# Interleaving the 512-column and 256-column matmuls of each block product, contraction tile by contraction tile, in a one-core decoder block

## What is computed

```python
h = rms_norm(x, norm_mix_pre)
proj = einsum("btd,dp->btp", h, w_in) + b_in          # input projection, 2048 -> about 11 thousand columns
...                                                    # two recurrent branches, merge, output projection
x = x + rms_norm(mix_out, norm_mix_post)
h = rms_norm(x, norm_ffn_pre)
gate = causal_dwconv(einsum("btd,df->btf", h, ffn_w_gate), ffn_conv_w, ffn_conv_b)
up = einsum("btd,df->btf", h, ffn_w_up)
out = einsum("btf,fd->btd", gelu(gate) * up, ffn_w_down)
x = x + rms_norm(out, norm_ffn_post)
```

## Time and profile before

| | |
|---|---|
| median of three runs | 2742.39 us |
| span of the profiled execution | 2742.6 us |
| TensorE, matmuls | 2709.5 us busy (99%), 14435 instructions |
| TensorE, weight loads | 2315.1 us busy (84%) |
| DVE | 2051.3 us (75%) |
| ACT | 1366.2 us (50%) |
| GpSimd | 365.0 us (13%) |

### The profile page before, as it was taken

How to read it: one execution, slowest core, us unless ns; L and a number is a source line. 1 busy time by engine, 2 the same in 40 slices (tenths; PEclk the granted TensorE clock), 3 DMA queues, 4 the chain that set the end, 5 groups by cost and what they waited for, 6 DMA issues and landing times. The chain is left out here.

```text
span 2742.6 us, 39530 instructions
## 1 busy us (share of the span) xinstructions
PE 2709.5 (99%) x14435; PEld 2315.1 (84%) x14435; DVE 2051.3 (75%) x2374; ACT 1366.2 (50%) x1717; POOL 365.0 (13%) x438
## 2 busy tenths in 40 slices
PE   8999999999999999999989999999999999999998
PEld 7888888888888888888878888888888888888887
DVE  7788888888656554433688787878787888787888
ACT  4365555555543232223565555555555555555554
POOL 1000000000020010000001222222222222222213
PEclk9999999999999999999999999999999999999999
DMA  4344444445434334445625888888888888888876
GB/s 179 116 142 126 142 127 141 127 145 186 156 112 128 91 114 143 138 139 183 215 77 164 186 172 164 169 186 169 164 171 184 169 165 173 183 168 165 174 167 246
DMA packets 463086, 429.67 MB, mean 157 GB/s; under 512 B 14978, under 2 KB 359174, under 8 KB 460184
## 3 DMA queue, kind: packets, MB, share of 16 engines
q1 hardware_dynamic: 401208, 300.98, 36.2%
q0 software_dynamic: 51424, 108.72, 22.8%
q10 hardware_dynamic: 10368, 18.88, 1.8%
HBM read 315.28 MB, written 113.25 MB: 156 GB/s over the span
## 5 line engine op out<-in xcount | busy, mean ns | idle before, releaser
L1953 POOL DMA_DIRECT2D down_sums<-arena x304 | 261.2, 967 | 906.2 <-ACT arena L1688 881.2
L2580 DVE TENSOR_TENSOR sum_ring<-quads 128x1024 f32<-128x1024 f32 x164 | 201.0, 1226 | 169.1 <-PE ps L1139 137.1
L1644 ACT CAST op_ring<-sum_ring 128x1024 fp32r<-128x1024 f32 x164 | 173.0, 1055 | 269.3 <-DVE sum_ring L2580 269.3
L1133 PE MATMUL ps<-hl,op_ring 128*128 128x512 f32 x1064 | 266.1, 392 | 2.6 <-ACT hl L1622 1.6
L1997 DVE TENSOR_TENSOR w_lo<-raw,w_hi 128x2048 fp32r<-128x2048 f32 x68 | 155.7, 2290 | 150.3 <-ACT w_hi L1273 145.1
L1133 PEld LDWEIGHTS ps<-hl,op_ring 128*128 128x128 f32 x1064 | 193.3, 189 | 39.0 <-ACT hl L1622 1.8
L1273 ACT CAST w_hi<-raw 128x2048 fp32r<-128x2048 f32 x69 | 131.6, 1907 | 151.8 <-PE ps L762 108.0
L1688 ACT COPY arena<-ps 128x512 f32<-128x512 f32 x320 | 178.7, 585 | 51.3 <-PE ps L1174 42.9
L2594 DVE TENSOR_TENSOR op_ring<-sum_ring,op_ring 128x1024 fp32r<-128x1024 f32 x164 | 199.9, 1219 | 5.0 <-ACT op_ring L1644 5.0
L1133 PE MATMUL ps<-h,op_ring 128*128 128x512 f32 x792 | 198.0, 392 | 1.6 <-ACT h L1622 1.3
L1172 PE MATMUL ps<-op_ring,act_hi 128*128 128x512 f32 x480 | 187.6, 391 | 0.1
(11 more groups left out here) (394 smaller groups left out, 6043.2 us busy)
## 6 DMA issues: line engine op xcount, KB each, us to landing
down_sums<-arena POOLq DMA_DIRECT2D x320, 256.0 KB, 6.6
quads<-in_w_in SPq DMA_DIRECT2D x116, 512.0 KB, 4.4
quads<-in_ffn_w_gate SPq DMA_DIRECT2D x88, 512.0 KB, 4.7
quads<-in_ffn_w_up SPq DMA_DIRECT2D x88, 512.0 KB, 4.8
quads<-in_ffn_w_down SPq DMA_DIRECT2D x88, 512.0 KB, 7.6
raw<-in_w_in SPq DMA_DIRECT2D x30, 1024.0 KB, 5.5
raw<-in_w_out SPq DMA_DIRECT2D x24, 1024.0 KB, 5.0
projections<-arena ACTq DMA_DIRECT2D x40, 256.0 KB, 3.3
```

Source lines behind the costliest of these rows:

```text
L1133: pe.matmul(ps[:, bank, :], w[0][:, j, :], h[:, j, :, :].rearrange("p r t -> p (r t)"), start=(j == 0 and q not in (M7, M6)), stop=False, ...
L1644: act.copy(op_hi[slot], src).then_inc(op_hi_ready, 1)
L1953: pool.dma_start(dst, src, accum_op=ALU.add).then_inc(acc_added[s], 16)
L2580: dve.tensor_tensor(sum_of(i, pos), quads[:, a, :], quads[:, b, :], ALU.subtract if q in (M7, M6) else ALU.add).then_inc(weights_summed, 1)
```

## The change

In both places the eight long and eight short matmuls of a product are no longer two runs. For each tile `j` the long matmul is followed at once by the short one. The wait for `op_lo_ready` moves ahead of the first short matmul, which is now behind the first long one. The first seven products of the feed-forward keep the old order. No instruction is added or removed; `op_done` is counted up by the last matmul as before.

```diff
@@ in_product
                 for j in range(HALF):
                     pe.matmul(ps[:, bank, :], w[0][:, j, :], IN_MOVING[q](j), start=(j == 0 and q in (P1, P4, P6, P5)), stop=False,
                               skip_group_check=True)
-                pe.wait_ge(op_lo_ready, o + 1)
-                for j in range(HALF):
+                    if j == 0:
+                        pe.wait_ge(op_lo_ready, o + 1)
                     mm = pe.matmul(ps[:, bank, 0:TH], w[1][:, j, :], IN_MOVING[q](j)[:, 0, :], start=False, stop=(j == HALF - 1),
                                    skip_group_check=True)
@@ times_h
-                for j in range(HALF):
+
+                def by_hi(j):
                     pe.matmul(ps[:, bank, :], w[0][:, j, :], h[:, j, :, :].rearrange("p r t -> p (r t)"),
                               start=(j == 0 and q not in (M7, M6)), stop=False, skip_group_check=True)
-                for r in turned_between:
-                    less_hi(r)
-                pe.wait_ge(op_lo_ready, o + 1)
-                for j in range(HALF):
-                    mm = pe.matmul(ps[:, bank, 0:TH], w[1][:, j, :], h[:, j, 0, :], start=False, stop=(j == HALF - 1),
-                                   skip_group_check=True)
+
+                def by_lo(j):
+                    return pe.matmul(ps[:, bank, 0:TH], w[1][:, j, :], h[:, j, 0, :], start=False, stop=(j == HALF - 1),
+                                     skip_group_check=True)
+
+                if isinstance(i, int) and i == 0 and pos < len(SLOT_FIRST):
+                    for j in range(HALF):
+                        by_hi(j)
+                    for r in turned_between:
+                        less_hi(r)
+                    pe.wait_ge(op_lo_ready, o + 1)
+                    for j in range(HALF):
+                        mm = by_lo(j)
+                else:
+                    for j in range(HALF):
+                        by_hi(j)
+                        if j == 0:
+                            pe.wait_ge(op_lo_ready, o + 1)
+                        mm = by_lo(j)
                 mm.then_inc(op_done, 1)
```

## The result

The changed kernel takes 2761.73 us at the median of four runs (2759.95 to 2762.93), the kernel before 2742.61 us in the same comparison: a ratio of 1.0069 with a 95% interval of 1.0056 to 1.0081, 19 us slower. The recorded span is 2760.4 us. This is where the third rival, a stream that never settles, had the time: 2763 us, with a chance of 32%.

The account below looks back on a forecast made before the run. TensorE was taken to bound the kernel in both stretches. From 2742.6 us, 9.7 us less for the pitch of the pairs and 1.7 us more for the wait gave 2734.6 us, with a range of 2712 to 2764 us.

Parts of the forecast that it names:

- the third rival: Input projection and feed-forward: each long matmul pays 7 ns, no short discount; 353.7 ns a pair, 2763 us; chance 32%.
- The bound: Input projection and feed-forward: TensorE alone sets the pace, busy 571.00 of 571.00 and 1251.94 of 1252.00 us.
- Step 1: Alternating pairs in both stages: 346.7 ns a pair instead of 349.1, 9.7 us less over 4032 pairs.
- The weight load: Under the matmuls of both stages: a load of 104 ns fits under a settled short matmul, some 16 ns to spare.
- Step 2: Wait for the low part moved forward: free in mid-stage, 1.7 us more where the feed-forward fills its slots.
- The second: Rival for both stages: order doesn't matter, the pair keeps 349.1 ns, only the wait remains; 2744.3 us; chance 18%.
- The first rival: Both stages: long matmuls settle, every short one gets the discount; 340.7 ns a pair, 2710 us; chance 16%.

Follow-up runs that it names:

- mirrored: Against the kernel before, every second input-projection product starts with its short matmuls, as do feed-forward products behind short ones; 2737.65 us, ratio 0.9985.

## Why the prediction was wrong, point by point

- **The bound.** Right. TensorE sets the pace in both stretches, no wait takes its place, and only the pitch decides.
- **Step 1, the pitch of an alternating pair.** This is the step that failed. It bounded the pair by 340.7 and 353.7 ns and took 346.7; measured were 353.3 ns in mid-stage, just under the upper bound. Over 4032 pairs that is 4032 x (353.3 - 349.1) = 17 us more where 9.7 us less were forecast. A smaller error sits in the base: 349.1 ns was read in the input projection and used for all pairs, though a product behind a down operation cost only 2.77 us, 346 ns a pair; that is part of why the ledger above has 18.1 us. The pitch of 346.7 ns does occur, in one product between two stops, but it isn't the state of the stream mid-stage. The reason given for the choice, that one short matmul should upset the long stream less than eight do, was argued and not shown by any row. The row that spoke against it was on the table, as the case for the third rival: the discount is gone with the second short matmul. The other reason, that both first-of-run pitches and both settled ones give about 347 ns, took two coincident numbers as support for each other. First-of-run pitches were those of a stream that had settled in a run before; in the alternating stream no such run exists. The runs of 2 and of 4 show how little a pitch by place in the run says: 2.786 and 2.806 us a product where this reckoning gave 2.804 and 2.802.
- **The weight load.** The prediction held that a load fits under a short matmul with 16 ns to spare, and that loads and covers are as many as before. The count is right, the conclusion isn't: halving the load under the short matmul takes the pair from 353.3 to 340 ns. A load that fits under a matmul by its length can still cost. The Trainium skill (TensorE: Matmul & The Clock Gate, section Back-to-back issue gap) gives the gap of an isolated matmul from its own columns alone. By that the order would make no difference; five orders of the same instructions gave 2.783 to 2.827 us a product here, so the measurement decides.
- **Step 2, the wait.** Right in kind and place: it is free in mid-stage and shows only where the slots fill. Its size was forecast as 1.7 us; the changed kernel shows 2.1 us of idle time in three stops (two were forecast) and the run with the wait alone 0.3 us. The stretch in which it falls grew by 1.0 us in the changed kernel and is 1.2 us shorter than before in the run with the wait alone, so its price is below what these single traces can tell.
- **The rivals.** The third had the kind and the size: 353.7 ns a pair and 2763 us against 353.3 and 2761.73. Its two parts are each off by 2 to 3 ns the other way, so that the sum is nearer than the parts: it had the long matmuls 7 ns above the settled pitch and the short ones at 120 ns, and they are 9 ns above it (236) and at 117. The second (order doesn't matter) is refuted by the runs. The first rival's pair (340.7 ns) appears only with smaller loads or a shorter second matmul, at 340 ns.
- **What remains open.** Why the cost is not monotone in the length of the run, why the alternating stream ran at 346 ns in one product early in the feed-forward and at 353.3 mid-stage, and what in the engine lets a covered load cost anything. A pair of unlike lengths with 384 columns showed that even the old order has an excess there. The runs narrow it to load and stream together; they don't show the mechanism.

## What to carry to other kernels

Where TensorE is busy without a gap, the order of long and short matmuls is a term of its own: here five orders of the same instructions lie 44 ns apart in a product of 2.8 us, 22 us over the kernel's 504 products. Finest interleaving was the worst of them; merging runs over the border of two products had the lowest cost a product, though its time can't be told from that of runs of 2. The number of turns doesn't rank the orders: runs of 2 have four turns where runs of 8 have one, and they are faster. Don't build an estimate for a mixed stream from pitches taken at the turns of a grouped one: time one stage in the new order and read the starts.

## What the runs showed of the hardware that I had not expected

| order or size | us a product | in units of 16 clocks at 2.4 GHz (6.667 ns) |
|---|---|---|
| runs of 1 | 2.827 | 424 |
| runs of 2 | 2.786 | 418 |
| runs of 4 | 2.806 | 421 |
| runs of 8 (before) | 2.793 | 419 |
| runs of 16 (mirrored) | 2.783 | 417.5 |
| runs of 8, low weights halved | 2.753 | 413 |
| runs of 8, both loads halved | 2.760 | 414 |
| runs of 8, all matmuls 512 columns | 3.627 | 544 |

All are means over the input projection; the rounding of its starts to 0.1 us leaves some 0.1 units. The unit is chosen because it fits: within the rounding a product comes out in whole units at the mean, or two products do where the pattern spans two, and three alternating pairs take 159 units (1.06 us). That the engine works in such units is not shown by anything else. The settled long matmul is 34 units (226.7 ns) for 32 units of columns, the settled short one 18 (120 ns) for 16, and with the halved load beneath it 17.
